# One token per sample in a recurrent mixer: the outer products of two heads in row quarters of TensorE, and the states as the moving side in its column quarters

## The reference

```
f = lb + (1 - lb) * sigmoid(hf);  k = 1 - f;  q = hq * HG_SCALE
S = f[:, None] * S0 + outer(k, v)          # state, 128 x 128, an output of the layer
o = q @ S                                  # read of the new state
o = rms_norm(o, hg_norm_g) * silu(hg)
```

## Time and profile before

| | us |
|---|---|
| median of 3 runs | 2141.13 |
| the three runs | 2132.35, 2141.13, 2143.48 |
| the profiled execution | 2131.16 |
| its span | 2129.5 |

### The profile page before, as it was taken

How to read it: one execution, slowest core, us unless ns; L and a number is a source line. 1 busy time by engine, 2 the same in 40 slices (tenths; PEclk the granted TensorE clock), 3 DMA queues, 4 the chain that set the end, 5 groups by cost and what they waited for, 6 DMA issues and landing times. The chain is left out here.

```text
span 2129.5 us, 40340 instructions
## 1 busy us (share of the span) xinstructions
PE 1978.9 (93%) x16626; PEld 1771.3 (83%) x16626; DVE 879.6 (41%) x1690; ACT 589.2 (28%) x1192; POOL 155.4 (7%) x214
## 2 busy tenths in 40 slices
PE   5899889999949599897999999999999999999997
PEld 4667665565645598887999999999999999999997
DVE  6233035556502257742223334545335524442453
ACT  5133146555502123422212222211112111111121
POOL 4000101100030023420000000000000000000000
PEclk8899979999979699987999999999999999999999
DMA  8422443000072611212222113211111111111112
GB/s 234 66 68 77 201 120 101 1 2 1 2 210 91 231 33 34 52 41 63 75 85 71 40 50 90 60 50 42 47 50 49 32 57 50 40 46 52 44 31 97
DMA packets 164658, 148.30 MB, mean 70 GB/s; under 512 B 7681, under 2 KB 152018, under 8 KB 163586
## 3 DMA queue, kind: packets, MB, share of 16 engines
q1 hardware_dynamic: 153444, 123.77, 19.3%
q0 software_dynamic: 6208, 17.67, 3.3%
q10 hardware_dynamic: 4864, 4.84, 0.9%
HBM read 120.54 MB, written 29.99 MB: 71 GB/s over the span
## 5 line engine op out<-in xcount | busy, mean ns | idle before, releaser
L247 PE MATMUL psum<-xgl,t_wh 128*128 128x344 f32 x1056 | 338.2, 320 | 0.0
L246 PE MATMUL psum<-xgh,t_wh 128*128 128x344 f32 x1056 | 338.0, 320 | 0.0
L248 PE MATMUL psum<-xgh,t_wl 128*128 128x344 f32 x1056 | 337.3, 319 | 0.0
L247 PEld LDWEIGHTS psum<-xgl,t_wh 128*128 128x128 f32 x1056 | 198.6, 188 | 0.1
L248 PEld LDWEIGHTS psum<-xgh,t_wl 128*128 128x128 f32 x1056 | 198.4, 188 | 0.0
L246 PEld LDWEIGHTS psum<-xgh,t_wh 128*128 128x128 f32 x1056 | 198.2, 188 | 0.1
L248 PE MATMUL psum<-hh,t_wl 128*128 128x344 f32 x528 | 169.0, 320 | 0.0
L246 PE MATMUL psum<-hh,t_wh 128*128 128x344 f32 x528 | 168.9, 320 | 0.0
L247 PE MATMUL psum<-hl,t_wh 128*128 128x344 f32 x528 | 168.8, 320 | 0.0
L518 DVE TENSOR_TENSOR t_wl<-t_raw,t_wh 128x1024 fp32r<-128x1024 f32 x100 | 122.0, 1220 | 34.3 <-ACT t_wh L466 29.2
L466 ACT ACTIVATE t_wh<-t_raw 128x1024 fp32r<-128x1024 f32 x75 | 79.1, 1055 | 205.9 <-PE psum L248 205.9
(11 more groups left out here) (428 smaller groups left out, 3796.5 us busy)
## 6 DMA issues: line engine op xcount, KB each, us to landing
t_raw<-in_w_gate SPq DMA_DIRECT2D x22, 512.0 KB, 3.8
t_raw<-in_w_up SPq DMA_DIRECT2D x22, 512.0 KB, 3.8
t_raw<-in_w_down SPq DMA_DIRECT2D x24, 384.0 KB, 3.5
cmp_pages<-in_cache_kv SPq DMA_DIRECT2D x64, 128.0 KB, 2.2
t_raw<-in_w_in SPq DMA_DIRECT2D x16, 512.0 KB, 4.1
raw_n<-in_w_in SPq DMA_DIRECT2D x24, 256.0 KB, 3.5
r_raw<-in_w_in SPq DMA_DIRECT2D x12, 512.0 KB, 3.9
xh_copy<-xh SPq DMA_DIRECT2D x1, 4128.0 KB, 13.3
```

Of the source, the lines that this page charges most:

```text
L246: pe.matmul(out, wh, xh, start=(first and k == 0), stop=False)
L247: pe.matmul(out, wh, xl, start=False, stop=False)
L248: mm = pe.matmul(out, wl, xh, start=False, stop=(last and k == n - 1))
```

## The change

The samples' part of the mixer is laid out anew.

1. The keys `k8c` get 32 columns a head, 8 used and the rest cleared, so that one transpose of 128 x 128 puts head h's keys on rows 32h to 32h+7; ACT copies 128 x 128.
2. The values come by four small transfers into the same row quarters (`v8`, cleared by POOL first; SP waits for that), and POOL masks all heads at once, 128 x 1024, in slot 10. The four per-head masks of slots 44 to 47 are gone.
3. `sample_outer` runs in slots 47 and 50, each for two heads, whose products alternate between two row quarters of PE. In the same slots DVE is as before; it updates one head per slot in 47 to 50.
4. `sample_read` runs in slots 51 and 54, each for two heads. The query, repeated over 32 columns, is the stationary side and the state moves; the outcome is 32 equal rows in one of four column quarters, and four samples in a row use the four quarters.
5. New: a copy of 128 x 512 on ACT (slot 51) and on DVE (slot 54), and 8 transposes on PE (slots 55, 56) bring the outcome back to columns. The sums move from slot 56 to 57.

```diff
@@ sync @@
-            for tt in range(NTT):
-                n = rows(tt)
-                sp.dma_start(v[0:n, tt, :], c.hv_dram[tt * P:tt * P + n, :]).then_inc(v_in, 16)
+            for tt in range(NCH):
+                sp.dma_start(v[:, tt, :], c.hv_dram[tt * P:(tt + 1) * P, :]).then_inc(v_in, 16)
+            sp.wait_ge(cleared, 2)
+            for h in range(NH):
+                sp.dma_start(v8[32 * h:32 * h + NS, :], c.hv_dram[SEQ:NT, h * P:(h + 1) * P]).then_inc(v8_in, 16)
@@ tensor @@
-                for h in range(NH):
-                    mm = pe.transpose(c.psum[0:NS, X, h * P:(h + 1) * P], k8c[:, h, :], c.ident[:, :])
-                mm.then_inc(k8_t, 1)
+                pe.transpose(c.psum[:, X, 0:P], k8c[:, :, :].rearrange("p h s -> p (h s)"), c.ident[:, :]).then_inc(k8_t, 1)
...
+            def sample_outer(h0):
...
+                else:
+                    pe.wait_ge(new_state, NS * h0)
                 for j in range(2):
-                    mm = pe.matmul(c.psum[:, X + 2 * ((h + 1) % 2) + j, :], k8[:, h * P:(h + 1) * P], vm[h % 2][:, j * 512:(j + 1) * 512],
-                                   start=True, stop=True)
+                    for h in (h0, h0 + 1):
+                        r32 = slice(32 * h, 32 * h + 32)
+                        mm = pe.matmul(c.psum[:, X + 2 * ((h + 1) % 2) + j, :], k8[r32, :], vm[r32, j * 512:(j + 1) * 512],
+                                       start=True, stop=True)
...
+            def sample_read(h0):
+                pe.wait_ge(new_state, NS * (h0 + 2))
+                if h0 == 0:
                     pe.wait_ge(logged, NH)
-                for s in range(NS):
-                    mm = pe.matmul(c.psum[:, O, h * NS + s:h * NS + s + 1], ss[h][:, s * P:(s + 1) * P], q8[:, h, s:s + 1], start=True, stop=True)
+                for h in (h0, h0 + 1):
+                    for s in range(NS):
+                        g0 = 32 * (s % 4)
+                        at0 = (2 * (h % 2) + s // 4) * P
+                        mm = pe.matmul(c.psum[g0:g0 + 32, O + h0 // 2, at0:at0 + P], q8[:, h, s:s + 1].to_broadcast([P, 32]),
+                                       ss[h][:, s * P:(s + 1) * P], start=True, stop=True)
...
+            def turn_read(half):
+                pe.wait_ge(read_v if half else read_a, 1)
+                for x in range(4):
+                    mm = pe.transpose(c.psum[:, X + half, x * P:(x + 1) * P], sq[:, half * 512 + x * P:half * 512 + (x + 1) * P], c.ident[:, :])
+                mm.then_inc(read_t, 1)
...
-                if 47 <= j < 51:
-                    sample_outer(j - 47)
-                if 51 <= j < 55:
-                    sample_read(j - 51)
-                if j == 56:
+                if j in (47, 50):
+                    sample_outer(0 if j == 47 else 2)
+                if j in (51, 54):
+                    sample_read(0 if j == 51 else 2)
+                if j in (55, 56):
+                    turn_read(j - 55)
+                if j == 57:
                     sample_sums()
@@ scalar @@
-                if j == 55:
-                    act.wait_ge(read, NH)
+                if j == 51:
+                    act.wait_ge(read, 1)
+                    act.activation(sq[:, 0:512], c.psum[:, O, :], ACT.Copy).then_inc(read_a, 1)
+                if j == 56:
+                    act.wait_ge(read_t, 2)
@@ gpsimd @@
+            pool.memset(v8[:, :], 0.0).then_inc(cleared, 1)
+            pool.memset(k8c[:, :, :], 0.0).then_inc(cleared, 1)
...
-                if 44 <= j < 48:
-                    masked_values(j - 44)
+                if j == 10:
+                    masked_values()
@@ vector @@
+                if j == 54:
+                    dve.wait_ge(read, 2)
+                    dve.tensor_copy(sq[:, 512:1024], c.psum[:, O + 1, :]).then_inc(read_v, 1)
```

More of the change, by code:

```diff
@@ L1149, in recurrent_mixer @@
     k = c.low("r_k", [P, 2, NT])
-    v = c.low("r_v", [P, NTT, HG])
+    v = c.low("r_v", [P, NCH, HG])
+    v8 = c.low("r_v8", [P, P])
     raw = c.low("r_raw", [P, 2, KD, P])
@@ L1164, in recurrent_mixer @@
     ss3 = c.low("r_ss3", [P, SEQ])
-    vma = c.low("r_vm", [NS, SEQ])
+    vm = c.low("r_vm", [P, SEQ])
     fine = c.low("r_fine", [P, 4, 32])
     coarse = c.low("r_coarse", [P, 2, 16])
-    f8, k8c, q8, g8 = (c.low("r_" + x, [P, NH, NS]) for x in ("f8", "k8c", "q8", "g8"))
-    k8 = kd[0:NS, 0:4, :].rearrange("p c x -> p (c x)")
+    f8, q8, g8 = (c.low("r_" + x, [P, NH, NS]) for x in ("f8", "q8", "g8"))
+    k8c = c.low("r_k8c", [P, NH, 32])
+    k8 = kd[:, 0, :]
     o8, s8, r8 = (c.low("r_" + x, [P, NH * NS]) for x in ("o8", "s8", "r8"))
@@ L1174, in recurrent_mixer @@
     ss = [f[:, 0, 0:SEQ], k[:, 0, 0:SEQ], q[:, 0, 0:SEQ], ss3[:, :]]
-    vm = [vma[:, :], pm[0:NS, :, :].rearrange("p l x -> p (l x)")]
     w_in = [c.sem(f"r_w_in{i}") for i in range(2)]
@@ L1188, in recurrent_mixer @@
         c.sem("r8_" + x) for x in ("small", "k8_t", "k8", "vm", "outer", "state", "read", "o8", "sum", "log", "root", "n"))
+    cleared, v8_in, read_a, read_v, read_t = (c.sem("r8_" + x) for x in ("cleared", "v8_in", "read_a", "read_v", "read_t"))
     HB = 72
@@ L1287, in update @@
                 if h == 0:
-                    pe.wait_ge(v_in, 16 * NTT)
+                    pe.wait_ge(v_in, 16 * NCH)
                 for ch in range(NCH):
@@ L1312, in sample_keys @@
                 pe.wait_ge(fine_done, NH)
-                for h in range(NH):
-                    mm = pe.transpose(c.psum[0:NS, X, h * P:(h + 1) * P], k8c[:, h, :], c.ident[:, :])
-                mm.then_inc(k8_t, 1)
[L1317 to L1320, removed]
+                pe.transpose(c.psum[:, X, 0:P], k8c[:, :, :].rearrange("p h s -> p (h s)"), c.ident[:, :]).then_inc(k8_t, 1)
+            def sample_outer(h0):
+                if h0 == 0:
+                    pe.wait_ge(k8_done, 1)
+                    pe.wait_ge(vm_done, 1)
@@ L1321, in sample_outer @@
                     pe.wait_ge(at_done, 7 * NH)
                     pe.wait_ge(coarse_done, NH)
-                if h >= 2:
-                    pe.wait_ge(new_state, NS * (h - 1))
+                else:
+                    pe.wait_ge(new_state, NS * h0)
                 for j in range(2):
-                    mm = pe.matmul(c.psum[:, X + 2 * ((h + 1) % 2) + j, :], k8[:, h * P:(h + 1) * P], vm[h % 2][:, j * 512:(j + 1) * 512],
-                                   start=True, stop=True)
-                mm.then_inc(outer, 1)
@@ L1330, in sample_read @@
-            def sample_read(h):
-                pe.wait_ge(new_state, NS * (h + 1))
-                if h == 0:
-                    pe.wait_ge(logged, NH)
-                for s in range(NS):
-                    mm = pe.matmul(c.psum[:, O, h * NS + s:h * NS + s + 1], ss[h][:, s * P:(s + 1) * P], q8[:, h, s:s + 1], start=True, stop=True)
-                mm.then_inc(read, 1)
+                    for h in (h0, h0 + 1):
+                        r32 = slice(32 * h, 32 * h + 32)
+                        mm = pe.matmul(c.psum[:, X + 2 * ((h + 1) % 2) + j, :], k8[r32, :], vm[r32, j * 512:(j + 1) * 512],
+                                       start=True, stop=True)
+                        if j:
+                            mm.then_inc(outer, 1)
@@ new lines, in sample_read @@
+            def sample_read(h0):
+                pe.wait_ge(new_state, NS * (h0 + 2))
+                if h0 == 0:
+                    pe.wait_ge(logged, NH)
+                for h in (h0, h0 + 1):
[4 more added lines that the diff above has]
+                                       ss[h][:, s * P:(s + 1) * P], start=True, stop=True)
+                mm.then_inc(read, 1)
@@ L1460, in slot @@
                     act.wait_ge(upd, NH)
-                    act.activation(k8, c.psum[0:NS, X, :], ACT.Copy).then_inc(k8_done, 1)
-                if j == 55:
-                    act.wait_ge(read, NH)
-                    act.activation(o8[:, :], c.psum[:, O, 0:NH * NS], ACT.Copy).then_inc(o8_done, 1)
-                    act.activation(s8[:, :], c.psum[:, O, 0:NH * NS], ACT.Square).then_inc(o8_done, 1)
+                    act.activation(k8, c.psum[:, X, 0:P], ACT.Copy).then_inc(k8_done, 1)
+                if j == 51:
[3 more added lines that the diff above has]
+                    act.wait_ge(read_t, 2)
+                    turned = c.psum[:, X:X + 2, :].rearrange("p b (x j r) -> p (b x) j r", x=4, j=4)[:, :, :, 0]
+                    eight = lambda x: x[:, :].rearrange("p (x j) -> p x j", j=4)
+                    act.activation(eight(o8), turned, ACT.Copy).then_inc(o8_done, 1)
+                    act.activation(eight(s8), turned, ACT.Square).then_inc(o8_done, 1)
             high(0)
@@ L1481, in _ @@
         def _(pool):
+            pool.memset(v8[:, :], 0.0).then_inc(cleared, 1)
+            pool.memset(k8c[:, :, :], 0.0).then_inc(cleared, 1)
             pool.memset(at[:, :, :], 0.0).then_inc(zeroed, 1)
+            pool.wait_ge(cleared, 2)
             def keys(h):
@@ L1489, in keys @@
```

(7 more changed lines are left out.)

## The result

The changed kernel takes 2122.94 us (median of 5 runs, 2117.99 to 2126.03), the one before 2141.45 us (5 runs); the ratio is 0.9922, 95% interval 0.9896 to 0.9947. In a second set on another occasion it was 2120.77 against 2141.93, ratio 0.9909 (0.9882 to 0.9936). Forecast were 2121 us and a range of 2108 to 2133. Two executions that ran much slower at a lower clock (2335.03 us of outer_only, 2784.79 us of the kernel before beside it) are left out of all medians and ratios.

The account below looks back on a forecast made before the run. PE, busy 93% of the span, was taken as the bound; 4.1 us saved until the stall plus 15.1 behind it, 19.2 together, took the median from 2141.13 to 2122; 2121 was predicted, range 2108 to 2133.

Parts of the forecast that it names:

- Outer products: Slots 47 to 50 on PE: two calls of 2.0 us replace 7.64 us, 3.6 saved, plus 0.2 for one interruption less.
- Keys and masks: Ahead of the outer products: three transposes and POOL's four per-head masks go, 0.3 us saved, bounds 0 and 1.0.
- Reads, transposes, interruptions: PE behind the stall: reads 1.7 us instead of 13.65, eight transposes added at 0.85, interruptions of half steps at 0.65.
- the reading that only two quarters work at once: Reads on PE: if products start strictly in program order, 53 ns a record, 3.4 us in all, 1.7 us worse.
- The clock: PE behind the stall: falls in the stall, rises 5.5 us after the restart, 2.75 us lost, bounds 0 and 3.7.
- What brings the clock back: PE behind the restart: dense column-quarter reads, then three half steps without interruption, were to raise the clock after 5.5 us.
- the sum: PE's whole stretch: 4.1 us saved until the stall and 15.1 from restart to last product, together 19.2 us.
- A: PE behind the restart: the clock stays low until the stage ends, only 3.5 us gained, 2138 us; chance 0.07.
- B: Packed products: row quarters run in turn or column quarters two at a time or worse; gain 11 to 15 us, 2128; chance 0.12.
- C: Reads of the kernel before: its profiled execution is unlucky, others regain the clock sooner; gain 7.9 us, 2133; chance 0.10.
- D: From 753 to 937: moved work brings new clock falls, up to 15 us each; two give 2152 us, slower; chance 0.03.
- a low stretch between 753 and 937: Heads' levels, where the clock was at 1.00 before: a low stretch there would show the forecast wrong.

Follow-up runs that it names:

- outer_only: The changed kernel with the reads, copies and sums of the kernel before, one head in each of slots 51 to 54; 2123.78 us, ratio to before 0.9906.
- one_quarter: The changed kernel with outer products one head after the other and reads quarter by quarter, four in a row in one column quarter; 2122.23 us (one run).
- reads_only: The kernel before with the new reads, copies, transposes and their slots; outer products, keys and masks as before; 2125.48 us, ratio to before 0.9906.
- one_head_a_slot: The changed kernel with one head's outer product in each of slots 47 to 50, four records a call; 2125.02 us (one run).
- before_early_log: The kernel before with ACT's logarithm and exponential of head 3 in slot 50 instead of 51, which removes the stall; 2122.55 us, ratio to before 0.9904.
- after_early_log: The changed kernel with ACT's logarithm and exponential of head 3 in slot 50 instead of 51; 2118.00 us, ratio to before 0.9915.
- before_again_a and _b: The kernel before, profiled twice more without any edit; 2140.17 and 2140.81 us (one run each).
- two_read_slots: The kernel before with its one-column reads in slots 51 and 54, two heads in each; 2134.20 us, ratio to before 0.9948.
- after_again: The changed kernel once more, without any further edit; 2120.77 us, ratio to before 0.9909.

## Why the prediction was right, and where it was not

- **Outer products**: 3.8 us forecast with the lost interruption, and from the first of them to the stall 935.35 - 917.57 = 17.8 us before against 13.56 now; 4.2, of which 0.4 came with distances between half steps. The row halves of another stage gave the right price for quarters.
- **Keys and masks**: 0.3 us forecast, nothing came. Three transposes did go (0.35 us from the first to the next work before, 0.03 now), but the states of head 3 on DVE come no sooner, and PE waits for them that much longer. From the transposed keys of head 3 to the first outer product there were 917.57 - 904.94 = 12.63 us and are 931.77 - 919.12 = 12.65. PE waits 0.48 us for DVE's states where it waited 0.16, and DVE's instruction of 1.93 us, just ahead of the states, takes 1.93 without POOL's mask too, so the mask had not slowed it. The term that failed is the wait: PE's own work was not what bounds this place.
- **Reads, transposes, interruptions**: 18.45 us of work at full clock forecast behind the restart, 18.5 measured. Inside it the reads are 2.0 instead of 1.7 and the transposes 0.7 instead of 0.85. The form in the samples' attention was the right row; the reading that only two quarters work at once is refuted (1.01 us for 32 records, 32 ns each, where it had 53), and so is its ground, a start strictly in program order: the trace of one_quarter shows records started out of it.
- **The clock**: the mis-sized step. I let it fall in the stall and charged 2.75 us. In both profiled executions of the changed kernel it did not fall at the reads; in reads_only and one_head_a_slot, with the same stall and reads, a fall of 3.4 us cost 1.5. So even where it fell the charge was too high by 1.2 us.
- **What brings the clock back** was attributed wrongly. I put it on the dense reads and the three half steps without a break. outer_only has neither and gets it back; before_early_log never loses it at the reads. Of the 20.4 us, before_early_log and after_early_log, both at full clock at the reads, show what the layout is worth by itself: 239.6 - 231.5 = 8.1 us. The other 12.3 are the clock: 13.9 at the reads (36.3 against 22.4 from read to end), less the 1.5 of the short fall that only the changed kernel's profile has. Taking out the stall gives the same 12.3 and 3.1 of the stall.
- **How near the sum came is in part luck.** It had 4.1 until the stall and 15.1 behind it. Measured are 4.2 and 36.3 - 18.55 = 17.75, and 1.5 go the other way through the short fall near 902, which the sum did not have. The clock's 2.75 too much and those 1.5 too little offset each other in part.
- **Rivals**: A did not occur. B is refuted for the orders used. C, the accident, is refuted by three executions of three. D: a low stretch between 753 and 937 was named as a sign of being wrong, and there is one, 902.45 to 905.86; but before_again_a and _b have it too, so it is not shown to be the change's. D's price of 15 us a fall did not come, it cost 1.5.
- **The 10 us between the profiled execution and the median** lie ahead of the mixer: from the span's start to the mixer's first POOL instruction the profiled one of before was at 1.2 GHz for 119.5 us, the twelve others, of whatever kernel, for 136.5 to 153.6, and their mixers start 5 to 13 us later. The median was the right basis. The stage lost 20.4 us and the median 18.5, and the forecast of 20 lies between.

Open is why a stall of the same 3.06 us is followed by 27 to 31 us at 1.2 GHz in before, by 3.4 in outer_only, and by nothing in the changed kernel. The ten profiles with the stall show two patterns.

- Whether it falls goes with the outer products ahead of the stall. Where they stand one head to a slot (before three times, reads_only, two_read_slots, one_head_a_slot), the clock falls between 1.0 us ahead of the restart and 1.1 behind it, six of six. Where they stand in two slots, it does not fall (changed, after_again, one_quarter) or, with one-column reads, 1.8 us behind the restart (outer_only).
- How long it stays low goes with what follows the fall. Where a half step begins within 0.1 us of it (outer_only, reads_only, one_head_a_slot), it lasts 3.4 us; in two_read_slots' second fall, inside half steps without a break, as well. Where one-column reads follow (before, and the first fall of two_read_slots), it lasts until 5.3 to 5.7 us into a dense stretch, 10 to 31 us in all.

So the changed kernel may owe its undisturbed clock to where the stall falls in time and not to its products. No experiment moved only that, and neither pattern is shown to be a cause.

## What to carry to other kernels

When a change near a stall of a few us moves the time more than its own instructions can, look at the granted clock behind the stall, and try the kernel before without the stall: here two lines gave 15.4 us of the stage, and the rebuilt products 20.4, of which 8.1 are their own. Price packed products by a row of the same form in the same trace; both such prices held to 0.3 us (2.0 against 1.91, 1.7 against 2.0). Taking work off an engine saves nothing where it waits for another one next: look at the wait behind it, too. Compare stages and not whole executions when they start at different times.

## What the runs showed of the hardware

- Four column quarters in turn: 32 records of 128 columns in 1.01 us at full clock; the same records quarter by quarter, four products each, 2.36 us.
- Two row quarters in one call: eight records of 512 columns in 1.91 us (1.92 with one head after the other in the program); four alone also 1.91. Records of different quarters start out of program order (one_quarter, 942.14 to 942.25).
- Products of one moving column on a 128 x 128 f32 stationary side: 16 records in 1.70 us at full clock and 3.41 at half.
- Reads of one column between half steps of 1.88 us ran at 1.00 where no stall stood ahead of them (before_early_log), and also behind a stall once the clock was back (outer_only, from 947.3 on); behind a stall of 3.06 us they ran at 0.50 for 27 to 31 us in before.
